# Two fp32r passes for the prompt's attention scores, in a one-layer streaming encoder step

## The reference, cut to what matters

```python
# mixer A: 8 heads x 64, each chunk of 64 queries sees its own chunk and 8 before it
sc = einsum('bcqhd,bckhd->bchqk', chunked(q), k_band) * (d ** -0.5)
sc = where(valid, sc + bias, -inf);  p = softmax(sc);  o = einsum(p, v_band)
# mixer B: 8 heads x 64, each query sees the 256 keys that an indexer picked (all causal ones where fewer)
sc = einsum('bqhd,bqkhd->bqhk', q, kg) * (d ** -0.5)
p = softmax(where(valid, sc, -inf));  o = einsum(p, vg)
```

## Time and profile before

| | |
|---|---|
| median of 3 runs | 2730.73 us (2730.59 to 2732.59) |
| the profiled execution | 2731.63 us, span 2730.0 us, mean granted clock 0.98 |
| busy, share of the span | PE 95%, DVE 49%, ACT 36%, POOL 19% |

### The profile page before, as it was taken

The page is one execution under the profiler, slowest core; times in us unless marked ns, Lnnn a source line. Parts: engine busy times, 40 slices in busy tenths (PEclk is TensorE's granted clock), DMA queues, the critical chain, the costliest instruction groups (busy, mean ns, idle before and its releaser), DMA issues. The chain is left out here.

```text
span 2730.0 us, 40373 instructions
## 1 busy us (share of the span) xinstructions
PE 2598.7 (95%) x16684; PEld 2328.1 (85%) x16684; DVE 1341.8 (49%) x2433; ACT 986.6 (36%) x1671; POOL 510.8 (19%) x369
## 2 busy tenths in 40 slices
PE   7999999999998999987999999989799999999997
PEld 6999999988878799976777776658799999998886
DVE  6433232335543498977788733323732323333544
ACT  6333323234332323234666532221523333323432
POOL 0233333200001021750000000000134333310000
PEclk9999999999999999998999999999899999999999
DMA  3122222266632122214002315451122212145553
GB/s 124 49 82 65 82 66 90 76 261 217 216 127 67 51 97 69 66 51 143 28 28 102 124 64 177 169 185 47 55 82 65 82 64 82 65 154 215 204 201 123
DMA packets 153109, 294.28 MB, mean 108 GB/s; under 512 B 14032, under 2 KB 90456, under 8 KB 152928
## 3 DMA queue, kind: packets, MB, share of 16 engines
q1 hardware_dynamic: 146688, 268.12, 28.7%
q0 software_dynamic: 6240, 23.59, 2.4%
HBM read 237.26 MB, written 61.78 MB: 110 GB/s over the span
## 5 line engine op out<-in xcount | busy, mean ns | idle before, releaser
L803 DVE TENSOR_TENSOR f_dl<-f_raw_d,f_dh 128x2048 fp32r<-128x2048 f32 x66 | 151.3, 2293 | 273.6 <-ACT f_dh L619 273.6
L619 ACT ACTIVATE f_dh<-f_raw_d 128x2048 fp32r<-128x2048 f32 x66 | 126.5, 1916 | 321.2 <-PE f_pV L151 293.0
L569 ACT ACTIVATE f_gh<-f_pX 128x256 f32<-128x256 f32 x120 | 49.3, 411 | 321.1 <-PE f_pX L151 321.1
L1994 ACT ACTIVATE t_sc<-t_sc,t_small 128x640 f32<-128x640 f32 (+8 forms) x136 | 99.9, 735 | 152.3 <-DVE t_small L1923 117.5
L150 PE MATMUL f_pX<-f_xop,f_u_shi 128*128 128x256 f32 x504 | 149.2, 296 | 0.0
L151 PE MATMUL f_pX<-f_xop,f_u_slo 128*128 128x256 f32 x504 | 149.2, 296 | 0.0
L149 PE MATMUL f_pX<-f_xop,f_u_shi 128*128 128x256 f32 x504 | 149.2, 296 | 0.0
L149 PE MATMUL w_pw<-i_hi,r_T_hi 128*128 128x256 f32 (+1 forms) x504 | 145.3, 288 | 2.6 <-PEq L351 2.6
L150 PE MATMUL w_pw<-i_lo,r_T_hi 128*128 128x256 f32 (+1 forms) x504 | 144.7, 287 | 0.0
L151 PE MATMUL w_pw<-i_hi,r_T_lo 128*128 128x256 f32 (+1 forms) x504 | 144.2, 286 | 0.0
L150 PE MATMUL f_pX<-f_xop,f_g_shi 128*128 128x256 f32 x480 | 142.1, 296 | 0.0
(11 more groups left out here) (374 smaller groups left out, 8325.9 us busy)
## 6 DMA issues: line engine op xcount, KB each, us to landing
f_raw_d<-in_ffn_w_down SPq DMA_DIRECT2D x66, 1024.0 KB, 5.0
hid<-f_gh SPq DMA_DIRECT2D x22, 1152.0 KB, 8.8
f_raw_h<-hid SPq DMA_DIRECT2D x66, 384.0 KB, 5.6
f_g_raw<-in_ffn_w_gate SPq DMA_DIRECT2D x21, 1024.0 KB, 5.3
f_u_raw<-in_ffn_w_up SPq DMA_DIRECT2D x21, 1024.0 KB, 6.4
proj<-w_stage POOLq DMA_DIRECT2D x12, 1152.0 KB, 5.6
i_raw<-in_w_in SPq DMA_DIRECT2D x12, 1024.0 KB, 5.1
f_x<-in_x_prompt SPq DMA_DIRECT2D x16, 512.0 KB, 7.1
```

The lines of the kernel that those rows point to most:

```text
L569: act.activation(dst, by_tile(pX[:, c, 0:N[c]]), ACT.Copy).then_inc(s_copy, 1)
L619: act.activation(d_hi[slot(q)][:], raw_d[slot(q)][:], ACT.Copy).then_inc(s_dhi, 1)
L803: dve.tensor_tensor(d_lo[slot(q)][:], raw_d[slot(q)][:], d_hi[slot(q)][:].bitcast(F32), ALU.subtract)
L1994: act.activation(sc_of(g, 0, n) if len(src.shape) == 2 else in_halves(sc_of(g, 0, n)), src, ACT.Exp, bias=small[:, 1, g % 4:g % 4 + 1], ac ...
```

## The change

Keys come as high and low parts in fp32r: ScalarE rounds the keys of one head to 64 partitions, VectorE writes what is left to the other 64, each in two 64-partition instructions. Queries are loaded with each head's 64 columns twice, so that their transpose has the same query on both halves of the partitions; ScalarE rounds the high part, VectorE subtracts the low one. A score is then two fp32r matmuls for each run of keys, first the high part of the queries, then the low part, both against high and low keys together.

```diff
+                elif e[0] == "keys":                       # DVE
+                    dve.wait_ge(s_ma, misc[("k", x, t)] + 1)
+                    for r in range(2):
+                        i = dve.tensor_tensor(keys_of(x, t, r, 1 - r), turned_keys(r), keys_of(x, t, r, r).bitcast(F32), ALU.subtract)
+                    i.then_inc(s_ml, 1)
+                elif e[0] == "queries":
+                    dve.wait_ge(s_ma, misc[("q",) + e[1:]] + 1)
+                    dve.tensor_tensor(q_lo[:, hs, :], pm[:].rearrange("p (h c) -> p h c", c=P),
+                                      q_hi[:, hs, :].bitcast(F32), ALU.subtract).then_inc(s_ml, 1)
...
-                    act.activation(kT[x][:, :, t * P:(t + 1) * P], pm[:].rearrange("p (f c) -> p f c", c=P), ACT.Copy).then_inc(s_ma, 1)
+                    if x == 0 and t >= RING:               # ACT
+                        act.wait_ge(s_s, H * (t - 1))
+                    for r in range(2):
+                        i = act.activation(keys_of(x, t, r, r), turned_keys(r), ACT.Copy)
+                    i.then_inc(s_ma, 1)
...
-                    if h == 0:                             # PE
-                        pe.wait_ge(s_ma, misc[("q", x, t)] + 1)
+                    if h % 4 == 0:
+                        pe.wait_ge(s_ml, lo_n[("q", x, t, h // 4)])
...
-                    for c in range(0, nb, 4):
-                        last = pe.matmul(ps[g % 2][:, c * P:c1 * P], qT[:, (x * NP + t) % 2, h, :], kT[x][...], start=True, stop=True)
+                    for a, b, k in key_chunks(x, t):
+                        for q in (q_hi, q_lo):
+                            last = pe.matmul(ps[g % 2][:, a * P:b * P], q[:, h, :], key_rows(x, h, k, k + b - a),
+                                             start=q is q_hi, stop=q is q_lo)
```

Queries come in two halves of four heads, transposed at heads 4 and 6 of the tile before; for the first tile, the second half at head 1. Keys move from behind head 1's score to the front of head 0:

```diff
-plan = [("keys", 0, 0), ("queries", 0, 0), ("score", 0), ("score", 1)]
+plan = [("keys", 0, 0), ("queries", 0, 0, 0), ("score", 0), ("score", 1)]
...
-        if h == 4 and n + 1 < len(tiles):
-            plan.append(("queries",) + tiles[n + 1])
+        if h == 0 and n + 1 < len(tiles):
+            plan.append(("keys",) + tiles[n + 1])
+        if h in (4, 6) and n + 1 < len(tiles):
+            plan.append(("queries",) + tiles[n + 1] + (h // 2 - 2,))
+        if g == 1:
+            plan.append(("queries", 0, 0, 1))
```

The reduction gives the negated score and its minimum, so that the negation goes (in the samples for mixer A alone); the exponential takes its input with scale -1, and the bias is stored times 8:

```diff
-                    dve.tensor_tensor_reduce(..., scale=1.0, scalar=GONE, op0=ALU.add, op1=ALU.max, accum_out=small[:, 0, ...]).then_inc(s_mx, 1)
-                    dve.wait_ge(s_mx, g + 1)
-                    dve.tensor_scalar(small[:, 1, ...], small[:, 0, ...], -1.0, None, ALU.mult).then_inc(s_sc, 1)
+                    dve.tensor_tensor_reduce(..., scale=-HD ** -0.5, scalar=FIRST, op0=ALU.add, op1=ALU.min, accum_out=small[:, 0, ...]).then_inc(s_mx, 1)
```

More of the change, by code:

```diff
@@ L1203, in _ @@
                 sp.wait_ge(s_put[i], 16 * 2)
-            for j in range(2):
-                sp.dma_start(head.rows[:, j, :], proj_v[:, 0, (1 - j) * H * HD:(2 - j) * H * HD]).then_inc(head.s_row, 16)
+            sp.dma_start(head.rows[:, 0, :], proj_v[:, 0, H * HD:2 * H * HD]).then_inc(head.s_row, 16)
+            for e in range(2):
+                sp.dma_start(head.rows[:, 1, :].rearrange("p (h e d) -> p e h d", e=2, d=HD)[:, e],
+                             proj_v[:, 0, 0:HT * HD].rearrange("p (h d) -> p h d", d=HD)).then_inc(head.s_rq, 16)
             for i in range(2):
@@ L1572, in attn_plan @@
             plan.append(("score", g + 2))
-        if h == 1 and n + 1 < len(tiles):
-            plan.append(("keys",) + tiles[n + 1])
         if g >= 1:
@@ L1582, in attn_plan, with key_chunks @@
     return heads, plan
+RING = LEFT // 2 + 2
+KS0_HALF = 4 * RING * P
+def key_chunks(x, t):
+    first, n = blocks_of(x, t)
+    cuts = [c for c in range(n) if c % 4 == 0 or x == 0 and (first + c) % RING == 0] + [n]
+    return [(a, b, (first + a) % RING if x == 0 else first + a) for a, b in zip(cuts, cuts[1:])]
 def sample_plan(n):
@@ L1728, in attn_phase @@
             if e[0] in ("keys", "queries"):
-                order += [((e[0][0],) + e[1:], 0)]
+                order += [((e[0][0],) + e[1:], 1)]
             elif e[0] == "out":
@@ L1763, in _, with query_rows @@
             tiles = [(x, t) for x in range(2) for t in range(NP)]
+            def query_rows(n, half):
+                x, t = tiles[n]
+                c = x * N_QKV + half * FW // 2
+                for e in range(2):
+                    sp.dma_start(q_rows(n, half).rearrange("p (h e d) -> p e h d", e=2, d=HD)[:, e],
+                                 proj_v[:, t, c:c + FW // 2].rearrange("p (h d) -> p h d", d=HD)).then_inc(s_rq[half], 16)
             def rows_of(n):
                 x, t = tiles[n]
-                if n:
-                    sp.wait_ge(s_mf, misc[("q",) + tiles[n - 1]] + 1)
                 c = x * N_QKV
+                sp.wait_ge(s_mf, misc[("k",) + tiles[n - 1]] + 1)
                 sp.dma_start(rows[:, 0, :], proj_v[:, t, c + FW:c + 2 * FW]).then_inc(s_row, 16)
-                sp.dma_start(rows[:, 1, :], proj_v[:, t, c:c + FW]).then_inc(s_row, 16)
+                for half in range(2):
+                    sp.wait_ge(s_mf, misc[("q",) + tiles[n - 1] + (half,)] + 1)
+                    if half and n == NP + 1:
+                        sp.wait_ge(s_mx, NP * H)
+                    query_rows(n, half)
             def values(x):
@@ L1820, in _ @@
                 sp.dma_start(dst, proj[r0:r1, c:c + FW]).then_inc(s_out, 16)
-            sp.wait_ge(s_o, NH)
             sp.wait_ge(s_s, NH)
-            new_values(0)
-            new_values(1)
+            for s in range(2):
+                cached_values(s)
+                new_values(s)
             for s in range(2, len(items) + 1):
@@ L1990, in _, with act_exp @@
                     i.then_inc(s_ml, 1)
[L1992 to L1994 removed]
+        def act_exp(act, g, n, src, sign, total):
+            act.activation(sc_of(g, 0, n) if len(src.shape) == 2 else in_halves(sc_of(g, 0, n)), src, ACT.Exp, bias=small[:, 0, g % 4:g % 4 + 1], scale=sign, accum_out=total).then_inc(s_p, 1)
         @block.scalar
         def _(act):
[L1998 removed]
             for e in plan:
```

124 lines of the change are left out of this document (74 added, 50 removed).

## The result

The changed kernel took 2779 us (median of three; 2775.8 to 2781.3) against 2731 before: ratio 1.0171, 95% interval 1.0157 to 1.0184, some 47 us slower. The forecast was 2740 with a range to 2753: the sign was right, the size was not. A fourth execution, slow at 4269.9 us with a mean granted clock of 0.554, is left out. The profiled execution took 2775.8 (span 2774.3).

What follows compares the result with a forecast made beforehand. TensorE was taken to lead most of the kernel, VectorE following and short tiles hanging on chains between engines; 2731.6 + 0.7 (tile sum) + 8.4 (clock) = 2740.7, so 2740 us, range 2715 to 2753.

Steps and rivals of the forecast that it cites:

- the clock's charge: TensorE's loss to a lower clock behind each tile's stand: 0.7 us in 12 tiles, +8.4; bounds 0 to 1.8 a tile.
- start: Up to the first tile's outputs: +2.0 for the first reduction's chain, +3.0 for the queries' second half; +5.0, bounds 2 to 7.
- rival 3: Every tile loses its clock: 14 x 1.8 = +25.2 us, 2756 to 2757; chance 0.06.
- The walk: Step-by-step timing of a five-block tile's head: osb ready at 7.27 us, TensorE standing from 5.08, a stand of 2.2.
- the sum: All tile length changes added, from the start to (1,7), without the clock: +0.7 us.
- the step: Assumed VectorE price of each new 64-partition subtraction: 0.6 us, taken from the 512-wide osb operation.
- sign: Named evidence in the five-block stretch: VectorE's busy share up to 17 or more of 20 us.
- Rival 2: Key subtractions find copies ready, osb isn't late: nine tiles win 1.47 more each, -12.5 us, 2718; chance 0.25.
- Rivals 1, 4 and 5: Clock holds, 2731, 0.24; query rows late in short tiles, 2743 or 2744, 0.03; fp32r passes no cheaper, 2760 and more, 0.02.
- The 39 us: TensorE's net relief over all tiles: 46 us from cheaper score passes less 7 for extra query transposes; said not to reach the end.

Runs made afterwards that it cites:

- e1_fill: Changed kernel with one score's passes repeated on TensorE ahead of its wait for the scaled outputs, in every tile but the first: 2750.3 us.
- b1_subtract: Kernel before with the next keys' plan entry at tile start and two unused VectorE subtractions ahead of the scaling of the outputs: 2762.6 us.
- e2_osb_first: Changed kernel with both key subtractions issued behind the scaling of the outputs on VectorE, from the third tile's keys on: 2725.6 us.
- e6_warm: e2_osb_first with 23 identity transposes, results unread, on TensorE in the first tile where it stood still: 2722.7 us.

## Why the prediction failed, step by step

Tile lengths against the kernel before, forecast (without the clock's charge) and measured:

| | start | (0,1) | (0,2) | (0,3) | (0,4) | (0,5) | (0,6) | (0,7) | (1,0) | (1,1) | (1,2) | (1,3) | (1,4) | (1,5) | (1,6) | (1,7) |
|---|---|---|---|---|---|---|---|---|---|---|---|---|---|---|---|---|
| forecast | 5.0 | 2.0 | 0.8 | 0 | -0.4 | -0.7 | -0.2 | 0 | 2.0 | 2.0 | 0.8 | 0 | -0.7 | -4.1 | -1.8 | -4.0 |
| changed | 9.2 | 3.7 | 4.0 | 3.4 | 0.8 | 4.7 | 3.2 | 6.0 | 2.9 | 3.3 | 4.4 | 3.2 | 4.4 | -1.2 | -1.0 | -4.0 |
| e1_fill | 8.9 | 2.3 | 3.2 | 1.9 | -0.8 | 0.1 | 0.4 | 1.3 | 2.9 | 2.2 | 2.3 | 0.8 | 0.1 | -4.4 | -2.6 | -2.1 |

- *The step that failed is the clock:* "Bounds 0 to 1.8 a tile ... I charge 0.7 in 12 tiles: +8.4". All 14 tiles lost it, as rival 3 had it; but a stretch was 7.0 us long on average (98.6 / 14), not 3.6, which is up to 3.5 us of TensorE's work a tile in place of 1.8. In time 28 us came back when the stand was filled, 2.0 a tile where 0.7 was charged, the fill's own cost already taken off. The Trainium skill, "TensorE: Matmul & The Clock Gate", section "HAM oscillation — how this bites in real kernels", tells of a kernel whose tiles each begin at the lower clock after a wait of some 3 to 5 us; this trace agrees in 14 tiles of 14, with stands of 2.05 to 4.13 us. The upper bound came from one stretch, in a kernel whose TensorE was full on both sides of it (6.0 of 6.0 us from 1500 to 1506, 7.0 of 7.0 from 1513 to 1520); I took a single example for a ceiling. Even rival 3, 2757, which charged that bound in all 14 tiles, is 22 us short.
- *The walk was right for the tile it was made for.* In tile (0,5) osb was ready 7.2 us after the end of the score that precedes the keys (1368.9 to 1376.1), forecast 7.27; TensorE stood 2.05, forecast 2.2. Carried over to all 14 tiles it was too short: the four tiles (0,4) to (0,7) stood 2.05 to 2.77, the other ten 2.2 to 4.1, 42.3 in all against 30.8 by the walk. Why it is longer there was not taken apart.
- *Without the clock* the sum was +0.7; with the stand filled, the last osb came 16.6 later than before (13.6 us of stands and, behind 1290, 17 us at the lower clock are still in that run). Of the difference 3.9 is the start, 8 the tiles of one to four blocks up to (1,3), 1.9 the fill's own passes in the last tile; the tiles of five to seven blocks came within 1.3 us of the forecast. The start is the second step that failed: its own upper bound was 7, and 9.2 was measured. The chain up to the first reduction was right (1.9 later, forecast 2.0); the other 7.3, forecast 3.0, stand between it and the first osb.
- *Prices.* Below, the first reduction on VectorE's timeline, and the groups by form of its new subtractions (count, busy us, mean ns, idle before): those for the keys took 689 ns each, those for the queries 691, the step 0.7 where I took 0.6. A head of five blocks, transposes, score and values, took TensorE 2.30 from the first start to that of the next head (last fence), as forecast (0.56 + 0.68 + 1.06), before 2.70. The first reduction came at 1269.26, forecast near 1269; the last tile is 4.0 shorter, as forecast. VectorE's share from 1340 to 1360 was 15.98 of 20, not the 17 or more that was named as a sign.

```profile
1269.26 0.29 DVE L1977 CUSTOM_DVE_ANT_0 t_sc<-t_ps,a_bias 128x128 f32<-128x128 f32 x1 [0.78 <-PE t_ps L2187]
```

```profile
L2005 DVE TENSOR_TENSOR t_q_lo<-t_pm,t_q_hi 128x512 fp32r<-128x512 f32 x32 | 22.1, 691 | 17.6 <-ACT t_q_hi L2078 17.3
L2000 DVE TENSOR_TENSOR t_kS<-t_pm,t_kS 64x512 fp32r<-64x512 f32 x32 | 22.0, 689 | 23.4 <-ACT t_kS L2070 23.2
```

```profile
1370.41 0.71 PE L2155 MATMUL t_pt<-r_ident,t_sc 128*128 128x128 f32 x5
1370.88 0.48 PE L2187 MATMUL t_ps<-t_kS,t_q_hi 128*128 128x512 f32 x1
...
1371.60 1.28 PE L2206 MATMUL t_po<-a_v,t_pT 128*128 128x64 f32 x10
1372.71 0.73 PE L2155 MATMUL t_pt<-r_ident,t_sc 128*128 128x128 f32 x5
```

- *Rival 2* (the subtractions find their copies ready) is refuted: VectorE waited 1.45 us before them on average, 1.1 without the first, which waited 6.4. *Rivals 1, 4 and 5* as well: the clock didn't hold; one short wait of 0.9 us on a load of rows was seen; the passes were cheap.
- *The 39 us* that TensorE saves were rightly not counted at the end: with the stand gone, the change in its best order is worth on the whole as much as the negation alone.

Open: why a lower stretch lasts 3.4 us in one tile and 10.2 in another, and what part of the start's 7.3 us behind the first reduction belongs to the second half of the queries; neither was tried apart.

## What to carry to other kernels

When an edit puts work into an engine's queue, look for the hand-off behind it on which TensorE waits at the end of a tile, and issue that hand-off first; here moving two subtractions behind one scaling was worth 53 us. It took 32 us of stands away: a stand of 2 to 4 us on TensorE cost more than its own length here, as the lower clock followed it, so a relief of TensorE that opens stands can be a loss. Fill the stand with work whose result nobody reads: if the kernel gets faster, the clock was the price.

## What the runs showed of the hardware

- A granted clock of 0.5 for 3.4 to 10.2 us at 14 of 14 stands of 2.05 to 4.13 us in the changed kernel, and at 6 of 13 stands of 1.00 to 3.50 us in b1_subtract. The kernel before showed it behind one pair of waits (1.08 and 1.10) and behind none of its other eight stands, of up to 1.28 us.
- 64-partition subtractions of 512 columns took 689 ns, as long as those of 128 partitions (691).
- The same program can lose the clock in a tile in one execution and keep it in another: (1,6) of e2_osb_first, behind a stand of 1.40 us, and of e6_warm, behind one of 1.33; the tile with the loss was 1.5 us longer.
